# One step of a hybrid decoder layer on one core: queries computed by thirds of the tokens with two sets of scores among them, a convolution that steps over the prompt alone, and whole output tiles stored

## The reference, cut to what matters

```python
# queries: 8 heads of 64 plain and 32 rotary components
q = (rmsnorm(cq, q_norm) @ w_q_up).reshape(B, T, N_HEADS, QK_NOPE + QK_ROPE)
# causal attention of the prompt, in blocks of 128 queries
s = (q_lat . c + q_rope . k_rope) * ATTN_SCALE ; p = softmax(where(kp <= qp, s, NEG_INF))
# depthwise causal convolution, 31 taps, 512 channels, over u_ext of every sequence:
#   prompt: 30 zeros and the 1024 rows u; a sampled sequence: 30 rows of state and 4 new rows
y = conv(u_ext, conv_w) + conv_b ; conv_o = silu(layernorm(y))
y_prompt = rmsnorm(xp, final_norm) ; y_sample = rmsnorm(xs, final_norm)
```

## Time and profile before

| | |
|---|---|
| median of three runs | 2627.33 us |
| the profiled execution's own time | 2627.26 us |
| its span, first to last instruction | 2625.5 us |
| TensorE busy | 2570.5 us (98%) |
| VectorE busy | 1215.0 us (46%) |
| ScalarE, GpSimd busy | 605.2 us, 734.1 us |
| mean granted TensorE clock | 0.994 of full speed |

### The profile page before, as it was taken

The page is one execution under the profiler, slowest core; times in us unless marked ns, Lnnn a source line. Parts: engine busy times, 40 slices in busy tenths (PEclk is TensorE's granted clock), DMA queues, the critical chain, the costliest instruction groups (busy, mean ns, idle before and its releaser), DMA issues.

```text
span 2625.5 us, 43184 instructions
## 1 busy us (share of the span) xinstructions
PE 2570.5 (98%) x17063; PEld 2414.9 (92%) x17063; DVE 1215.0 (46%) x1788; ACT 605.2 (23%) x1292; POOL 734.1 (28%) x445
## 2 busy tenths in 40 slices
PE   8999999999999999998998999999999999999999
PEld 7999999999999897666677999789999999999999
DVE  5332333332382447765778771446532232332346
ACT  4100100100130234555442330332210010110114
POOL 2233243233242242001110222013233334233333
PEclk9999999999999999999999999999999999999999
DMA  4111111111113123006463312331111111111112
GB/s 141 48 36 52 45 42 50 46 42 50 41 46 114 41 63 92 1 1 248 177 237 98 122 49 72 128 122 41 49 38 42 56 39 50 48 42 46 48 36 87
DMA packets 205573, 185.45 MB, mean 71 GB/s; under 512 B 8584, under 2 KB 192105, under 8 KB 202646
## 3 DMA queue, kind: packets, MB, share of 16 engines
q1 hardware_dynamic: 201343, 144.55, 17.9%
q0 software_dynamic: 3584, 37.75, 3.7%
q10 hardware_dynamic: 543, 1.69, 0.2%
HBM read 167.66 MB, written 12.52 MB: 69 GB/s over the span
## 4 chain that ended last, share of the span: by engine, by line
PE 57%; ACT 2%; DVE 2%; issue 1%; DMA 0%; ACTq 0%; DVEq 0%
PE ps L370 13%; PE ps L369 13%; PE ps L366 13%; PE ps L1610 2%; PE ps L1580 2%; PE ps L1625 1%; PE ps L1592 1%; PE ps L1713 1%; PE ps L1913 1%; PE ps L1783 1%; PE ps L1675 1%; PE ps L1893 1%; PE ps L1785 1%; DVE uy L2521 1%; ACT p_t L2126 1%
## 5 line engine op out<-in xcount | busy, mean ns | idle before, releaser
L366 PE MATMUL ps<-h_hi,w_hi 128*128 128x352 f32 x2832 | 918.1, 324 | 11.1 <-POOL w_lo L1305 6.4
L369 PE MATMUL ps<-h_lo,w_hi 128*128 128x352 f32 x2832 | 915.3, 323 | 0.0
L370 PE MATMUL ps<-h_hi,w_lo 128*128 128x352 f32 x2832 | 914.6, 323 | 0.0
L1299 POOL CAST w_hi<-w_raw 128x1024 fp32r<-128x1024 f32 x192 | 200.7, 1045 | 1504.2 <-issue 661.1
L366 PEld LDWEIGHTS ps<-h_hi,w_hi 128*128 128x128 f32 x2832 | 533.0, 188 | 15.2 <-issue 12.3
L369 PEld LDWEIGHTS ps<-h_lo,w_hi 128*128 128x128 f32 x2832 | 532.8, 188 | 1.4
L370 PEld LDWEIGHTS ps<-h_hi,w_lo 128*128 128x128 f32 x2832 | 533.0, 188 | 0.0
L1305 POOL TENSOR_TENSOR w_lo<-w_raw,w_hi 128x1024 fp32r<-128x1024 f32 x192 | 472.2, 2459 | 15.4
L370 PE MATMUL ps<-g_hi,w_lo 128*128 128x352 f32 x1056 | 340.9, 323 | 0.0
L369 PE MATMUL ps<-g_lo,w_hi 128*128 128x352 f32 x1056 | 340.4, 322 | 0.0
L366 PE MATMUL ps<-g_hi,w_hi 128*128 128x352 f32 x1056 | 339.4, 321 | 0.3
(11 more groups left out here) (319 smaller groups left out, 2736.6 us busy)
## 6 DMA issues: line engine op xcount, KB each, us to landing
w_raw<-in_ffn_w_gate SPq DMA_DIRECT2D x44, 512.0 KB, 3.8
w_raw<-in_ffn_w_up SPq DMA_DIRECT2D x44, 512.0 KB, 3.9
w_raw<-in_ffn_w_down SPq DMA_DIRECT2D x32, 384.0 KB, 3.4
w_raw<-in_ffn_w_down SPq DMA_DIRECT2D x32, 320.0 KB, 3.1
ring<-in_cache_mem_k SPq DMA_DIRECT2D x16, 512.0 KB, 4.3
ring<-in_cache_mem_v SPq DMA_DIRECT2D x16, 512.0 KB, 5.3
w_raw<-in_w_in SPq DMA_DIRECT2D x14, 512.0 KB, 3.9
x_keep<-x_res SPq DMA_DIRECT2D x1, 4224.0 KB, 12.5
```

The lines of the kernel that those rows point to most:

```text
L366: mm = pe.matmul(out, w_hi[:, slot, c0:c0 + m], hi, start=start, stop=False)
L369: pe.matmul(out, w_hi[:, slot, c0:c0 + m], lo, start=False, stop=False)
L370: return pe.matmul(out, w_lo[:, slot, c0:c0 + m], hi, start=False, stop=stop)
L1299: pool.tensor_copy(w_hi[:, s, 0:w], w_raw[:, s, 0:w]).then_inc(w_hi_done, 1)
```

## The change

1. `QG` is reordered: the twelve plain groups go third by third. TensorE issues the scores of set 0 ahead of group 14 and those of set 1 ahead of group 16; ScalarE takes the exponentials of set 0 ahead of evicting group 15 and those of set 1 ahead of evicting group 17. Groups 12 to 17 use banks 1, 3, 4, 5, 1, 3, so that banks 0 and 2 are left to the two sets. The wait for all evictions moves ahead of the scores of set 2. Set 1's probabilities lie in the second half of the first buffer.
2. A channel group of the convolution takes 35 steps: 31 taps over 1024 columns, and, as every ninth, 17th, 25th and 33rd step, a `sample_conv` for one of the four new tokens of all eight sequences. It is three VectorE instructions: a product of 8x31 inputs and taps, a sum over the 31, and the bias. `CONV_TOTAL` is 140, and the counts at the places of `conv_steps` are new.
3. All output tiles are stored whole, by 9 DMAs, each after both halves are scaled.

```diff
-        QG = [(True, r, tt) for r in range(2) for tt in range(NTT)] + [(False, i, tt) for i in range(4) for tt in range(NTT)]
+        QG = [(True, r, tt) for r in range(2) for tt in range(NTT)] + [(False, i, tt) for tt in range(NTT) for i in range(4)]
+        Q_BANK = [i % 6 for i in range(12)] + [1, 3, 4, 5, 1, 3]
+        Q_BEFORE = [max([j for j in range(i) if Q_BANK[j] == Q_BANK[i]], default=None) for i in range(len(QG))]
+        FIRST_SCORES = {14: 0, 16: 1}
+        FIRST_EXPS = {15: 0, 17: 1}
+        def probs(i):
+            return p_t[:, 0, 4 * P:8 * P] if i == 1 else p_t[:, i % 3, :]
-        CONV_TOTAL = 4 * (CONV_WIDTH + 1)
+        CONV_OPS = CONV_WIDTH + DEC_SEQ
+        CONV_SAMPLE_OPS = {8 * (t + 1): t for t in range(DEC_SEQ)}
+        CONV_TOTAL = 4 * CONV_OPS
...
# SyncE, the stores
-                if i < Y_WHOLE:
-                    sp.wait_ge(*past(y_dve, i + 1))
-                    sp.dma_start(dst, y_out[0:w, i, :]).then_inc(y_stored[0], 16)
-                    continue
-                sp.dma_start(dst[:, 0:512], y_out[0:w, i, 0:512]).then_inc(y_stored[0], 16)
                 sp.wait_ge(*past(y_dve, i + 1))
-                sp.dma_start(dst[:, 512:1024], y_out[0:w, i, 512:1024]).then_inc(y_stored[1], 16)
+                sp.dma_start(dst, y_out[0:w, i, :]).then_inc(y_stored[0], 16)
...
# TensorE
-            pe.wait_ge(q_ev, Q_EV[-1])
-            pe.wait_ge(rope_done, 2 * NTT)
-            pe.wait_ge(ropes_in, 16 * ROPE_DMAS)
-            scores(0)
+            for i in range(len(QG)):
+                if i == min(FIRST_SCORES):
+                    pe.wait_ge(q_ev, Q_EV[FIRST_HEADS])
+                    pe.wait_ge(rope_done, 2 * NTT)
+                    pe.wait_ge(ropes_in, 16 * ROPE_DMAS)
+                if i in FIRST_SCORES:
+                    scores(FIRST_SCORES[i])
+                q_group(i)
+                if 2 <= i < 2 + 2 * NTT:
+                    q_rotated(i - 2)
             for i in range(len(SETS) + 1):
-                if i + 1 < len(SETS):
+                if i == 1:
+                    pe.wait_ge(q_ev, Q_EV[-1])
+                if 1 <= i < len(SETS) - 1:
                     scores(i + 1)
...
# ScalarE, ahead of evicting group i
+                if i in FIRST_EXPS:
+                    exps(FIRST_EXPS[i])
...
# VectorE
+            CONV_TURNS = 3 * [1] + 3 * [3] + 10 * [5] + [3, 2, 2]
+            def sample_conv(j, t):
+                u = uy[:, j + 1, U_S0:US].rearrange("p (b w) -> p b w", b=DEC_BATCH)
+                taps = conv_w[:, j, :].unsqueeze(1).to_broadcast([P, DEC_BATCH, CONV_WIDTH])
+                y = uy[:, j, SEQ:T].rearrange("p (b w) -> p b w", b=DEC_BATCH)[:, :, t]
+                steps.mark(dve.tensor_tensor(conv_s[:, :, :], u[:, :, t:t + CONV_WIDTH], taps, ALU.mult))
+                steps.wait()
+                steps.mark(dve.tensor_reduce(y, conv_s[:, :, :], AX_X, ALU.add))
+                steps.wait()
+                dve.tensor_scalar(y, y, gains[:, G_CONVB + j:G_CONVB + j + 1], None, ALU.add).then_inc(cvs, 1)
...
-            conv_steps(8)
+            conv_steps(3)
...
             maxima(0)
+            conv_steps(1)
+            maxima(1)
+            conv_steps(2)
...
-                if i + 1 < len(SETS):
+                if 1 <= i < len(SETS) - 1:
                     maxima(i + 1)
-                    if i % 2 == 0:
-                        conv_steps(1)
+                if i + 1 < len(SETS) and i % 2 == 0:
+                    conv_steps(2 if i % 8 == 0 else 1)
...
-                conv_steps(1 if h < 4 else 2 if h < 6 else 4)
+                conv_steps(CONV_TURNS[h])
```

More of the change, by code:

```diff
@@ L1546, in q_group @@
                 rope, n, tt = QG[i]
-                if i >= 6:
-                    pe.wait_ge(q_ev, Q_EV[i - 5])
+                if Q_BEFORE[i] is not None:
+                    pe.wait_ge(q_ev, Q_EV[Q_BEFORE[i] + 1])
                 for k in range(3):
@@ L1552, in q_group @@
                     w = [x[:, k, c0:c0 + P] for x in (wq_hi, wq_lo)]
-                    out = ps[:, i % 6, 0:TT]
+                    out = ps[:, Q_BANK[i], 0:TT]
                     pe.matmul(out, w[0], hi, start=(k == 0), stop=False)
@@ L2101, in _, with exps @@
                               u_stage[b * DEC_SEQ:(b + 1) * DEC_SEQ, 1, :]).then_inc(cs_stored, 16)
+            def exps(i):
+                n = (SETS[i][0] + 1) * P
+                act.wait_ge(nm_done, i + 1)
+                if i >= 3:
+                    act.wait_ge(at_t, TURNS_BEFORE[i - 1 if i == 3 else i - 2])
+                half, first, _ = half_of(i)
+                if first and half >= 2:
+                    act.wait_ge(*sums_known(half - 2))
+                for g in range(len(SETS[i][1])):
+                    act.activation(probs(i)[:, g * n:(g + 1) * n], set_scores(i)[:, g, :], ACT.Exp,
+                                   bias=neg_max(i)[:, g:g + 1], scale=1.0, accum_out=row_sum(i, g)).then_inc(exp_done, 1)
             for i, (rope, n, tt) in enumerate(QG):
+                if i in FIRST_EXPS:
+                    exps(FIRST_EXPS[i])
                 cols = slice(tt * TT, (tt + 1) * TT)
@@ L2105, in _ @@
                 if rope:
[L2106 removed]
+                    act.activation(qr_raw[:, n, cols], ps[:, Q_BANK[i], 0:TT], ACT.Copy, scale=ATTN_SCALE).then_inc(q_ev, 1)
                     continue
@@ L2113, in _ @@
                 for g in range(2):
-                    act.activation(q_all[0:QK_NOPE, 2 * n + g, cols], ps[g * QK_NOPE:(g + 1) * QK_NOPE, i % 6, 0:TT],
+                    act.activation(q_all[0:QK_NOPE, 2 * n + g, cols], ps[g * QK_NOPE:(g + 1) * QK_NOPE, Q_BANK[i], 0:TT],
                                    ACT.Copy, scale=ATTN_SCALE).then_inc(q_ev, 1)
-            def exps(i):
-                n = (SETS[i][0] + 1) * P
-                act.wait_ge(nm_done, i + 1)
-                if i >= 3:
-                    act.wait_ge(at_t, TURNS_BEFORE[i - 2])
-                half, first, _ = half_of(i)
-                if first and half >= 2:
-                    act.wait_ge(*sums_known(half - 2))
-                for g in range(len(SETS[i][1])):
-                    act.activation(p_t[:, i % 3, g * n:(g + 1) * n], set_scores(i)[:, g, :], ACT.Exp,
-                                   bias=neg_max(i)[:, g:g + 1], scale=1.0, accum_out=row_sum(i, g)).then_inc(exp_done, 1)
             def probs_taken(i):
@@ L2514, in conv_steps @@
                                           ALU.mult, ALU.add).then_inc(cvs, 1)
-                        continue
-                    into = y
-                    if step % CONV_OPS == CONV_WIDTH:
-                        x, y = (uy[:, plane, U_S0:US].rearrange("p (b w) -> p b w", b=DEC_BATCH)[:, :, w0:w0 + DEC_SEQ]
-                                for plane, w0 in ((j + 1, w), (j, 0)))
-                        into = uy[:, j, SEQ:T].rearrange("p (b w) -> p b w", b=DEC_BATCH)
-                    dve.scalar_tensor_tensor(out=into, in0=x, scalar=conv_w[:, j, w:w + 1], in1=y, op0=ALU.mult,
-                                             op1=ALU.add).then_inc(cvs, 1)
+                    else:
+                        dve.scalar_tensor_tensor(out=y, in0=x, scalar=conv_w[:, j, w:w + 1], in1=y, op0=ALU.mult,
+                                                 op1=ALU.add).then_inc(cvs, 1)
                 conv_at[0] = min(conv_at[0] + n, CONV_TOTAL)
```

27 lines of the change are left out of this document (12 added, 15 removed).

## The result

The changed kernel takes 2613.16 us (median of four runs, 2612.23 to 2613.38) against 2628.4 us, the median of four runs of the kernel before beside it: a ratio of 0.9946, 95% interval 0.9934 to 0.9957. The forecast was 2615.7 us, its range 2611.5 to 2620.5. The profiled execution took 2613.38 us (span 2611.6), 13.9 us less than the one of before. One run of the kernel before beside experiments 5 to 8 took 6023 us, a slow one, and is counted in no ratio.

A forecast was written before the change was run, and what follows sets the result against it. TensorE, busy for 2570.5 of 2625.5 us, was taken as the bound, so only its waits and slow stretches could be won: -0.5 - 1.0 - 4.6 - 5.2 - 0.3 = -11.6 us on 2627.26 gives 2615.7 us, range 2611.5 to 2620.5.

The forecast's parts named there:

- A: First convolution steps ahead of the value evictions: shorter steps remove a 0.5 us TensorE wait, -0.5 us.
- B: Attention's start: one 2.3 us wait replaces 1.0 and 2.2; -1.0 us with a clock fall, -2.6 without.
- rival 1: Attention's start: the clock does not fall behind the new wait, 2614.1 us; chance 0.28.
- C: Last sequence's sums: wait shrinks from 3.15 to 1.25 us (-1.9) and half clock behind it goes (2.7): -4.6 us.
- D: Convolution's end: the 3.85 us wait for the last step and the half clock behind it go, -5.2 us.
- E: Output stores at the kernel's end: nine DMAs carry the same bytes, between 0 and -0.6 us, taken as -0.3.
- Rival 2: Waits at the last sums and last convolution step only shrink, clock still falls: 2619 to 2622 us; chance 0.14.
- Rival 3: Attention's start: early scores bring nothing because ScalarE's queue is longer, 2616.7 to 2618 us; chance 0.07.
- Rival 4: Sampled attention: VectorE becomes the bound; sample steps of 7 us would cost 18 us, 2634 us; chance 0.03.

The follow-up runs named there:

- experiment 5: Kernel before with only the query reordering and early scores, and 3 instead of 8 wide convolution steps ahead of the maxima, five moved to units 6 to 10: 2625.09 us.
- experiment 6: Kernel before with its wide convolution steps, only their turns moved earlier (5 in units 6 to 11, then 3, 2, 2 in the last three): 2620.14 us.
- experiment 7: Changed kernel with its narrow steps placed late, turns of 4 in units 6 to 10 and in the last three: 2619.68 us.
- experiment 8: Changed kernel with the product and sum of each sample step made eight times, same result: 2694.4 us.
- experiment 1: Kernel before with only the query reordering and early scores, eight wide convolution steps left ahead of the maxima: 2629.26 us.
- experiment 3: Kernel before with only the store change, nine whole stores: 2628.09 us.
- experiment 4: Changed kernel with ScalarE taking set 1's exponentials behind the last eviction instead of ahead of it: 2610.66 us.
- experiment 2: Kernel before with only the convolution change, six steps ahead of the first maxima: 2615.44 us.
- experiment 11: Changed kernel run again with nothing edited, for its spread and a second profile: 2611.52 us.
- experiment 12: experiment 4 plus an earlier third exponential for the last sequence's sums and last convolution turns of 2, 3, 2 instead of 3, 2, 2: 2609.39 us.

## Why the prediction was right, and where it was off

**A, the first steps (0.5; 0.50 in the marks).** The size is right between traces of one kind only. The wait for `v_all` was 0.45 us before and none after, but 1.2 us in the second profile of the changed kernel, and 1.7 us in experiments 1, 3 and 6, whose steps there are those of before. There are two courses. The view of one line's instructions shows them, first in the changed kernel's first profile, then in experiment 4, whose code is the same up to there:

```profile
L2504 DVE COPY u_new<-uy x4: 167/261/929, 981.6 to 982.8; 128x32 f32<-128x32 f32 x4
```

```profile
L2504 DVE COPY u_new<-uy x4: 361/993/997, 979.0 to 981.1; 128x32 f32<-128x32 f32 x4
```

Four small copies (minimum, median, maximum in ns) take 1.37 or 3.09 us, while GpSimd subtracts for `cq_lo` beside them, and the steps behind start that much later. In either course the narrow steps save 0.4 us of wait (0.45 to none, 1.7 to 1.2), half of the 0.8 us that the forecast had for the two steps. SBUF — State Buffer of the Trainium skill (SBUF: two separate sides) says that VectorE, in its modes that use two ports, and GpSimd share a port pair which the one that starts first holds for a whole instruction while the other is blocked. The trace of experiment 4 fits that: a slow copy of 32 columns takes 0.99 us, about as long as one of the subtractions beside it (0.94 us). No run here took GpSimd away, so the cause is not shown, nor why it is one course or the other.

**B, the start of the attention (1.0; 2.76).** The mechanism was right: a new wait of 2.29 us (forecast 2.3) for the last eviction in place of the two old ones. Without a fall 2.6 us were forecast, and 2.76 came. What did not hold is "I take the fall as the likelier": the clock did not fall in the profiled run, which is rival 1 (2614.1 us against 2613.16 measured), and it did in the second profile. With the fall B would have been 1.6 us (experiment 7 has the same code here and the fall, and takes 38.60 us for the stretch, from 1000.65 to 1039.25). Behind the waits of 1.0 and 2.2 us the clock fell in four of five profiles (both of before, experiments 3 and 6, not experiment 2), behind the one of 2.3 us in three of five (the second of the changed kernel, experiment 7 and the kernel with sample steps three times as long, not the first of the changed kernel and experiment 5). The price of a fall rests on a row that is not all half clock: the eight scores took 3.18 us in the earlier trace rows, and 3.78 in experiment 1. So this term was a choice between two values that the kernel does not settle, and it is in part luck that the sum came out near: 1.64 us were won here by a fall that did not come, and 0.98 lost at 1538 us by one that did. TensorE: Matmul & The Clock Gate of the Trainium skill (What's actually happening) has the chip's windows run free of the program, and the two profiles of each kernel agree: equal waits, other falls. What decides it at a given place no run here shows. A table load in front of evictions was no trouble: it takes 1.28 us, and the exponential starts 0.02 us behind it (1029.28). So the drain that the Trainium skill gives in ScalarE: Activation LUTs (What ACT_TABLE_LOAD costs) does not show here either.

**Between B and C (nothing; 0.85).** Costed at nothing and missed. Of the two waits for `nm_row` (0.8 us together) one of 0.3 is left in the changed kernel's list; a narrower step ahead of the row maxima ends sooner (1.28 instead of 1.56 us). The rest is open, but it is no accident of one pair: experiment 4's stretch agrees with the changed kernel's to 0.01 us (367.59 and 367.58), the second profile of before with the first to 0.06 (368.49 and 368.43). In the second profile of the changed kernel it is 366.71, with a mean clock of 0.86 from 1192 to 1204 us where the first has 0.72; before had 0.73 there, so the clock is not what won the 0.85. No wait came in the attention for the two steps at every eighth set.

**C, the sums (wait 1.9 and clock 2.7; 1.89 and 3.14).** As forecast, the third exponential is late next, and the wait is 1.26 us (forecast 1.25). The 16 matmuls behind it took 2.03 us instead of 3.76, and from the sums to the last 48 products it is 15.14 us in both profiles of the changed kernel, before 18.28 and 18.26: the 2.7 us of the forecast were 0.4 too low.

**D, the last step (5.2; 5.49).** No wait, and 4.90 us for the 16 matmuls that took 6.38. The two steps left ran at 1.65 us each beside GpSimd, as the stretched rate had it.

**Behind D (nothing; 0.98 back).** The wait at 1538 us cost a fall in this run. It is no wait of the change; I had its row and did not price it. The first profile of before was the exception there: of thirteen profiles (all but the one with sample steps eight times as long) ten have half clock at this place.

**E, the stores (0.3; 0.25).** Right, and 0.3 in experiment 3.

**Rivals.** Rival 2 is excluded: no fall behind the sums or the last step in either profile of the changed kernel. Rival 3 is excluded by B for the whole change. Part 1 alone does bring nothing, and for more than the reason that rival 3 gives: there VectorE's turn of eight steps keeps ScalarE waiting. Rival 4 was priced wrongly: steps of 7.2 us cost not 18 but 81 us. At the real 1.06 us it plays no part.

The sum of what I forecast was 11.6 us and the traces differ by 13.9; 1.76 of the missing 2.3 us is B. Of the 13.9 us some 5 are clock and not waits removed (1.64 in B, 3.14 in C, 1.5 in D, less 0.98); those of C and D go with the waits, those of B and the 0.98 change from run to run.

## What to carry to other kernels

Where filler work stands in front of something that TensorE waits for, ask for the length of the turn at that place and not for its average room: one line that moved six wide steps away from the last units brought 7 us, and cheaper steps left there kept waits of 1.8 and 2.2 us. An early issue on one engine pays only if each engine behind it is free at that moment: shorten its turn in the same edit, and test the parts together as well as alone. Where two profiles of the same kernel differ, compare stretches between marks, and count a stretch at half clock as the price of a wait that is not charged every time (the counts follow).

## What the runs showed of the hardware

- The kernel before spread over 8.1 us in 21 runs, the changed one over 3.5 us in nine, and experiment 4 over 0.5 us in five. But experiment 12, which has the waits of experiment 4 and a shorter one at the sums, spread over 4.6 us in five. So fewer waits alone do not give a narrow spread, and what sets it stays open.
- How often half clock followed a wait of TensorE, over thirteen profiles (all but the one with sample steps eight times as long): the 3.15 us at the sums and the 3.85 us at the last step, five of five each; 2.0 us at 789 us, thirteen of thirteen; the other one of 2.0 us, at 1551 us in the earlier trace rows, ten of thirteen; 2.29 us at the attention's start, three of five; 1.0 and 2.2 us one behind the other there, four of five; 1.26 to 1.30 us at the sums, none of five; 1.55 us once of once, 1.83 us not once of once. So length alone does not decide it.
- The fall at the attention's start cost 1.64 us behind the two waits (experiment 2 against before), and 0.9 or 1.2 us behind the one of 2.29 us (37.44 us for the stretch without it, 38.37 in experiment 11 and 38.60 in experiment 7 with it).
- Four VectorE copies of 128x32 took 1.37 or 3.09 us in the same code beside the same GpSimd work, and TensorE's wait for `v_all` was 1.2 us longer in the longer course.
